# Feed-forward token planes at one residue modulo 512 bytes, with a copied high part for the narrow products

## The reference

```python
def swiglu_ffn(h, w_gate, w_up, w_down):
    return (jax.nn.silu(h @ w_gate) * (h @ w_up)) @ w_down

for l in range(DEPTH):                     # DEPTH = 2, x is 256 tokens by 1024
    h = rms_norm_2(x, ffn1_norm[l])
    x = x + 0.5 * swiglu_ffn(h, ffn1_w_gate[l], ffn1_w_up[l], ffn1_w_down[l])
    ...                                    # mixer
    h = rms_norm_2(x, ffn2_norm[l])
    x = x + 0.5 * swiglu_ffn(h, ffn2_w_gate[l], ffn2_w_up[l], ffn2_w_down[l])
```

## Time and profile before

| | before |
|---|---|
| median of 3 runs | 2394.99 us (2394.8 to 2395.54) |
| the profiled execution | 2395.84 us |
| its span, first to last instruction | 2393.7 us |
| mean granted TensorE clock in the span | 0.999 |

### The profile page before, as it was taken

How to read it: one execution, slowest core, us unless ns; L and a number is a source line. 1 busy time by engine, 2 the same in 40 slices (tenths; PEclk the granted TensorE clock), 3 DMA queues, 4 the chain that set the end, 5 groups by cost and what they waited for, 6 DMA issues and landing times.

```text
span 2393.7 us, 34175 instructions
## 1 busy us (share of the span) xinstructions
PE 2371.1 (99%) x12542; PEld 2012.4 (84%) x12542; DVE 1877.3 (78%) x1961; ACT 1439.7 (60%) x1474; POOL 14.3 (1%) x34
## 2 busy tenths in 40 slices
PE   8999999999999999999999999999999999999998
PEld 7788899888888888888888888888888888897887
DVE  7767786678888888888889898677966677788766
ACT  6645455467777777777777776555254454544444
POOL 1000000000000000000000010000000000000000
PEclk9999999999999999999999999999999999999999
DMA  8375233459999999999999996853455666533663
GB/s 302 111 258 177 70 131 141 152 202 376 382 379 348 381 379 378 348 381 377 380 348 378 381 395 249 281 180 124 132 188 181 194 229 230 177 128 123 199 192 126
DMA packets 315953, 603.73 MB, mean 252 GB/s; under 512 B 9121, under 2 KB 135201, under 8 KB 315553
## 3 DMA queue, kind: packets, MB, share of 16 engines
q1 hardware_dynamic: 314160, 592.70, 69.9%
q10 hardware_dynamic: 1136, 7.87, 0.8%
q0 software_dynamic: 576, 2.10, 0.2%
HBM read 597.91 MB, written 8.91 MB: 254 GB/s over the span
## 4 chain that ended last, share of the span: by engine, by line
PE 94%; DVE 3%; ACT 1%; DMA 1%; DVEq 1%; issue 0%; SPq 0%; ACTq 0%
PE bank L217 20%; PE bank L219 19%; PE bank L218 19%; PE bank L1229 17%; PE bank L1234 8%; PE bank L3526 1%; PE bank L2968 1%; PE bank L3453 1%; PE bank L2243 1%; PE bank L2253 1%; DMA mslot<-in_e_w_in 1%; PE bank L2943 1%; PE bank L1727 1%; PE bank L1070 0%; PE bank L2162 0%
## 5 line engine op out<-in xcount | busy, mean ns | idle before, releaser
L3218 DVE TENSOR_TENSOR weights_lo<-mslot,weights_hi 128x2048 fp32r<-128x2048 f32 x336 | 767.5, 2291 | 112.8 <-ACT weights_hi L3111 112.1
L3111 ACT ACTIVATE weights_hi<-mslot 128x2048 fp32r<-128x2048 f32 x336 | 644.1, 1920 | 212.9 <-PE bank L219 212.8
L1229 PE MATMUL bank<-x_parts,weights_hi 128*128 128x512 f32 x1760 | 510.3, 393 | 1.9 <-DVE x_parts L933 1.9
L1383 DVE TENSOR_TENSOR weights_lo<-scratch,weights_hi 128x2048 fp32r<-128x2048 f32 x165 | 377.2, 2289 | 164.4 <-ACT weights_hi L1376 164.4
L1229 PEld LDWEIGHTS bank<-x_parts,weights_hi 128*128 128x128 f32 x1760 | 325.2, 188 | 71.3 <-DVE x_parts L933 2.4
L217 PE MATMUL bank<-weights_hi,x_parts 128*128 128x512 f32 x920 | 359.7, 391 | 1.0 <-DVE weights_lo L3218 0.7
L217 PE MATMUL bank<-weights_hi,x_pair 128*128 128x512 f32 x896 | 354.8, 396 | 0.2 <-issue 0.2
L219 PE MATMUL bank<-weights_hi,x_pair 128*128 128x512 f32 x896 | 349.8, 390 | 0.0
L218 PE MATMUL bank<-weights_lo,x_pair 128*128 128x512 f32 x896 | 349.3, 390 | 0.0
L218 PE MATMUL bank<-weights_lo,x_parts 128*128 128x512 f32 x888 | 346.1, 390 | 0.0
L1234 PE MATMUL bank<-x_parts,weights_lo 128*128 128x256 f32 x1760 | 343.3, 280 | 0.0
(11 more groups left out here) (551 smaller groups left out, 2625.2 us busy)
## 6 DMA issues: line engine op xcount, KB each, us to landing
mslot<-in_o_moe_w_gate SPq DMA_DIRECT2D x112, 1024.0 KB, 6.4
mslot<-in_o_moe_w_up SPq DMA_DIRECT2D x112, 1024.0 KB, 6.3
mslot<-in_o_moe_w_down SPq DMA_DIRECT2D x112, 1024.0 KB, 6.6
scratch<-in_ffn_w_gate SPq DMA_DIRECT2D x44, 1024.0 KB, 5.4
scratch<-in_ffn_w_up SPq DMA_DIRECT2D x44, 1024.0 KB, 5.4
scratch<-in_ffn_w_down SPq DMA_DIRECT2D x44, 1024.0 KB, 5.2
mslot<-in_o_w_in SPq DMA_DIRECT2D x7, 2048.0 KB, 10.6
scratch<-in_e_ffn_w_gate SPq DMA_DIRECT2D x11, 1024.0 KB, 5.4
```

The costliest lines, as they stand in the source:

```text
L1229: pe.matmul(m.ps[bank + j][:, :].rearrange("p (i t) -> p i t", i=2), hi[:, k, cols(j)], m.x_wide[k], start=(k == 0), stop=False)
L1383: dve.tensor_tensor(m.wlo[to][:, :], m.fslot[i], m.whi[to][:, :], ALU.subtract).then_inc(m.sig["f_lo"], 1)
L3111: act.activation(m.whi[(place + half) % PLACES][:, :], r.slot[slot + half], ACT.Copy).then_inc(s["r_hi"], 1)
L3218: dve.tensor_tensor(m.wlo[i][:, :], r.slot[slot + half], m.whi[i][:, :], ALU.subtract).then_inc(s["r_lo"], 1)
```

## The change

Block 0 stays as it is. For v = 1 to 4 the high plane begins at column `PIECE` = 2048, that is 192 bytes lower, so that both planes have residue 64. In these blocks ScalarE copies the high plane (eight groups of 256 columns) once, after up(0) and ahead of the high part for up(1), to two places at residue 256: three k to a free end of `mix_parts` and five k into `mslot3_parts`. The narrow products of gate(0), up(0) and gate(1) read the high plane (residue 64), those from up(1) on read the copy (residue 256). The stationary operand of the last unit's down product, which lies over the high plane, moves from residue 256 to 64 with it. The order of the products, the counts of products and all semaphores stay.

```diff
+PLANE_AT = [XH_AT] + 4 * [PIECE]
+COPY_SPLIT = 3
+COPY_FRONT, COPY_BACK = 11296, 560
@@ place
+        m.x_copy = [cut(m.mix, COPY_FRONT, COPY_SPLIT, SEQ),
+                    cut(mslot3_parts, KT * HALF + COPY_BACK, KT - COPY_SPLIT, SEQ)]
@@
-    planes = x_all[:, 0:2 * XH_AT].rearrange("p (i t) -> p i t", i=2)
-    m.x_wide = [planes[:, :, k * SEQ:(k + 1) * SEQ] for k in range(KT)]
-    m.f_xl, m.f_xh = cut(x_all, 0, KT, SEQ), cut(x_all, XH_AT, KT, SEQ)
+    planes = [x_all[:, 0:2 * at].rearrange("p (i t) -> p i t", i=2) for at in PLANE_AT]
+    m.x_wide = [[t[:, :, k * SEQ:(k + 1) * SEQ] for k in range(KT)] for t in planes]
+    m.f_xl, m.f_xh = cut(x_all, 0, KT, SEQ), [cut(x_all, at, KT, SEQ) for at in PLANE_AT]
@@ ffn_pe, inner
-            pe.matmul(..., hi[:, k, cols(j)], m.x_wide[k],
+            pe.matmul(..., hi[:, k, cols(j)], m.x_wide[v][k],
+        def narrow_tokens(u, k):
+            if v == 0 or isinstance(u, int) and (u == 0 or u == 1 and kind == "gate"):
+                return m.f_xh[v][:, k, :]
+            return m.x_copy[0][:, k, :] if k < COPY_SPLIT else m.x_copy[1][:, k - COPY_SPLIT, :]
-                last = pe.matmul(m.ps[bank + j][:, 0:SEQ], lo[:, k, cols(j)], m.f_xh[:, k, :],
+                last = pe.matmul(m.ps[bank + j][:, 0:SEQ], lo[:, k, cols(j)], narrow_tokens(u, k),
@@ ffn_hidden
-        pair = [t[:, KT - 2:KT, :].rearrange("p k t -> p (k t)") for t in (m.f_xh, m.f_xl)]
+        pair = [t[:, KT - 2:KT, :].rearrange("p k t -> p (k t)") for t in (m.f_xh[v], m.f_xl)]
@@ ffn_act
     up(0)
+    if v > 0:
+        act.activation(m.x_copy[0], m.f_xh[v][:, 0:COPY_SPLIT, :], ACT.Copy)
+        act.activation(m.x_copy[1], m.f_xh[v][:, COPY_SPLIT:KT, :], ACT.Copy)
+        act.drain()
     ffn_hi(act, m, v, "up", 1)
```

More of the change, by code:

```diff
@@ L933, in ffn_entry_low @@
         dve.scalar_tensor_tensor(m.f_xl[:, k, :], turned(m, u, k),
-                                 gain[:, k:k + 1], m.f_xh[:, k, :], ALU.mult, ALU.subtract).then_inc(s["n_xl"], 1)
+                                 gain[:, k:k + 1], m.f_xh[m.splits[u]][:, k, :], ALU.mult, ALU.subtract).then_inc(s["n_xl"], 1)
 def ffn_entry_dve(dve, m, u, gain, v, scale):
@@ L1027, in tokens @@
             act.wait_ge(s["n_tr"], rows_turned(m, u) + k // 2 + 1)
-            last = act.activation(m.f_xh[:, k, :], turned(m, u, k), ACT.Copy, scale=gain[:, k:k + 1])
+            last = act.activation(m.f_xh[m.splits[u]][:, k, :], turned(m, u, k), ACT.Copy, scale=gain[:, k:k + 1])
             if k % 2 == 1:
@@ L1228, in wide @@
         def wide(j, k):
-            pe.matmul(m.ps[bank + j][:, :].rearrange("p (i t) -> p i t", i=2), hi[:, k, cols(j)], m.x_wide[k],
+            pe.matmul(m.ps[bank + j][:, :].rearrange("p (i t) -> p i t", i=2), hi[:, k, cols(j)], m.x_wide[v][k],
                       start=(k == 0), stop=False)
+        def narrow_tokens(u, k):
+            if v == 0 or isinstance(u, int) and (u == 0 or u == 1 and kind == "gate"):
+                return m.f_xh[v][:, k, :]
+            return m.x_copy[0][:, k, :] if k < COPY_SPLIT else m.x_copy[1][:, k - COPY_SPLIT, :]
         def narrow(j, ks):
             for k in ks:
-                last = pe.matmul(m.ps[bank + j][:, 0:SEQ], lo[:, k, cols(j)], m.f_xh[:, k, :],
+                last = pe.matmul(m.ps[bank + j][:, 0:SEQ], lo[:, k, cols(j)], narrow_tokens(u, k),
                                  start=False, stop=(k == KT - 1))
@@ L1285, in down_part @@
         hi, lo = parts(ffn_place(v, "down", NU - 1 if final else None), D)
-        hh, hl = ffn_hidden(m, last=final)
+        hh, hl = ffn_hidden(m, v, last=final)
         cols, tok = slice(half * HALF, (half + 1) * HALF), slice(t * P, (t + 1) * P)
@@ L1335, in ffn_pe, with ffn_hidden @@
         norm_pe(pe, m, u_out, 0)
-def ffn_hidden(m, last):
+def ffn_hidden(m, v, last):
     if last:
-        pair = [t[:, KT - 2:KT, :].rearrange("p k t -> p (k t)") for t in (m.f_xh, m.f_xl)]
+        pair = [t[:, KT - 2:KT, :].rearrange("p k t -> p (k t)") for t in (m.f_xh[v], m.f_xl)]
     else:
@@ L1468, in hidden @@
     def hidden(u, last=False):
-        hh, hl = (flat(t) for t in ffn_hidden(m, last))
+        hh, hl = (flat(t) for t in ffn_hidden(m, v, last))
         for j, cols in enumerate(halves):
```

## The result

| | before | after |
|---|---|---|
| median (8 runs each, alternating) | 2395.38 us (2394.61 to 2396.08) | 2401.98 us (2401.00 to 2403.86) |
| ratio, 95% interval | | 1.0028 [1.0019, 1.0037] |
| span of the profiled execution | 2393.7 us | 2398.9 us |

The account below looks back on a forecast made before the run. TensorE fills the feed-forward blocks, so time is the sum of product pitches. Terms -4.1 (wide), -0.4 (last down), +0.6 (early narrow), others zero, sum to -3.9 us: 2394.99 to 2391.1, range 2387.6 to 2396.6.

Parts of the forecast that it names:

- Step (1): Wide products of gate and up, both planes at residue 64, take 0.2267 us each: 0.097 us saved per pair, 4.1 us.
- The second route: Check on the wide products' gain: mean durations 393 against down's 390 ns, 3 ns x 352 x 4 = 4.2 us.
- Step (2): Narrow products from up(1) on keep residue 256 and pitch 0.1156: zero, bounds 3.1 us saved or 2.9 us lost.
- C: Rival: the phase persists, pairs gain nothing, only the gate's opening run gains slightly: -0.2 us, 2394.8; chance 0.20.
- E: Rival: each wide-to-narrow meeting of residues 64 and 256 costs 0.0066 us: +4.6 us, 2399.6; chance 0.13.
- Step (3): Narrow products of gate(0), up(0), gate(1) go to residue 64: 192 products by 3 ns, 0.6 us lost.
- Step (4): Last down's stationary operand goes to residue 64: 24 products a block from 0.2310 to 0.2267, 0.4 us gained in four blocks.
- Step (5): ScalarE's copy ahead of up(1), about 2.1 us, is covered by idle time: cost nothing; other bound 8.8 us in all.
- Step (6): The entry's ScalarE writes of the high plane only change address: zero; a tenth on each would be 0.3 us a block.
- B: Rival: wide and narrow products all at their lowest pitch, 0.2267 and 0.1133: -7.0 us, 2388.0; chance 0.20.
- D: Rival: residue affects no pitch, as TensorE's two SBUF ports are independent: 0.0 us, 2395.0; chance 0.07.

Follow-up runs that it names:

- the run with the planes back: Changed kernel with the high plane of blocks 1 to 4 back at residue 256, copies kept: 2395.5 us beside 2395.68 for the kernel before, ratio 0.9999.
- The copy-less kernel: Changed kernel without the copy, both planes at residue 64, all narrow products reading the high plane: 2402.32 us, ratio 1.0028 to the kernel before.
- The residue scan: Six single runs with high plane, copies or low plane at other residues by block: 2400.93 to 2403.73 us, beside 2395.4 to 2395.6 for the kernel before.

## Why the prediction was wrong

**What bounds the kernel** was right: in these blocks the time is the sum of the pitches. So was the remark that something is carried from one product to the next; its reading as a phase between the reads of the moving operand and of the next weights is not shown by any run.

The group of wide products over the whole span hides what happened, as the earlier trace rows do for before:

```profile
L1234 PE MATMUL bank<-x_parts,weights_hi 128*128 128x512 f32 x1760 | 513.1, 394 | 1.9 <-DVE x_parts L938 1.9
```

394 ns where it was 393: a duration ends at a modelled end, and only the starts show the pitch.

**Step (1), wide products at 0.2267 everywhere, -4.1 us: the step that failed.** It took "the nearest row for that is down's 0.2267" as a property of the residue. Up's opening has 0.2267 before and after, with the high plane at 256 and at 64, so it told nothing of the pairs. The gate's opening went to 0.2322, not to 0.2267, and the pairs to 0.350 in place of 0.342. Where the step forecast 97 ns less for a gate and up, they take 108 ns more (11047 to 11155). In each term what was read off was one place of a cycle. The second route, 393 less 390 ns, compared durations, which don't show the pitch.

**Step (2), narrow products unchanged, 0 within 3 us either way.** The residue of their operand is unchanged and their pitch isn't: up's run went from 0.1133 to 0.1178, the upper of the two bounds, 9 x 4.4 = 40 ns of up's 63. (The two bounds, 3.1 and 2.9 us, are one term rounded in two ways: 32 products by 2.25 ns, 42 times, is 3.0.) The mistake was to price wide and narrow products apart, when the run freezes at the place where the pairs leave the cycle.

**Down behind a gate, which no step priced**, lost 45 ns in each of eight units a block and 19 ns in one, 1.5 us in four blocks. The prediction looked at the entry to down only in the rivals C and E, as a measure for something else. The question to ask was what follows each changed product.

**Step (3)**: the narrow products of the first three groups have a mean duration of 283 ns, as said, but a duration isn't a price. By the starts, a block comes 0.13 us later to its first down in blocks 1 and 2 and 0.16 in block 4, where 0.14 was forecast for narrow products alone; the wide ones have changed in it too, so the agreement is partly luck. (In block 3 a wait at the entry hides it.) **Step (4)**: the 20 down products at the end of block 2 take 1929.99 - 1925.46 = 4.53 us, as forecast, against 4.62 in the earlier trace rows. These are the row of the narrow products on `x_parts` in block 2 of the changed kernel, and the end of that block in order of time:

```profile
L1244 PE MATMUL bank<-x_parts,weights_lo 128*128 128x256 f32 x48 | 8.7, 283 | 0.0
```
```profile
1925.46 0.39 PE L222 MATMUL bank<-weights_hi,x_parts 128*128 128x512 f32 x1
...
1929.99 0.39 PE L224 MATMUL bank<-weights_hi,small_parts 128*128 128x512 f32 x1
```

**Step (5), the copy at nothing**, was right, and the run with the planes back shows it by itself. ScalarE, VectorE and TensorE in block 1:

```profile
1487.39 0.85 ACT L1429 ACTIVATE mix_parts<-x_parts 128x768 fp32r<-128x768 f32 x1
1488.13 1.27 ACT L1430 ACTIVATE mslot_parts<-x_parts 128x1280 fp32r<-128x1280 f32 x1
1489.52 1.92 ACT L1386 ACTIVATE weights_hi<-scratch 128x2048 fp32r<-128x2048 f32 x1
1491.95 2.28 DVE L1393 TENSOR_TENSOR weights_lo<-scratch,weights_hi 128x2048 fp32r<-128x2048 f32 x1
1497.88 2.20 PE L1234 MATMUL bank<-x_parts,weights_hi 128*128 128x512 f32 x9
```

The copy takes 2.1 us, the high part behind it ends at 1491.44 (1491.9 was said), VectorE takes it up at 1491.95, and up(1) begins with no idle time before it. **Step (6)** has nothing in the traces against it.

**The rivals.** E had the sign and nearly the price: 16 x 0.0066 = 0.106 us per gate and up, measured 63 + 45 = 108 ns. It fell short of the 6.6 us mainly by down. But its mechanism, a price for each meeting of 64 and 256, is not what happens. The copy-less kernel has no such meeting and costs 148 ns. And the cost doesn't follow their number: with 8, 7, 6, 5 and 4 pairs the changed layout has 18, 16, 14, 12 and 10 meetings of a wide product and the narrow one behind it per gate and up, and costs 95, 108, 64, 64 and 20 ns over before's 11047. The number was a coincidence, and at 0.13 the chance was too low for a change of phase, which can go either way. C was right that a phase persists, and wrong that it would leave things as they are. B's state, all at the lowest, occurs in no run.

D, that residues have no effect, is refuted: one high plane at 64, 128, 192 or 256 gives 11195, 11171, 11227 or 11047 ns for the same 32 wide and 32 narrow products, each narrow one reading that plane. The Trainium skill, SBUF — State Buffer, section "Who interferes with whom", has TensorE's port for the moving operand and its port for weight loads as independent. The prediction took from that that no residue changes a pitch. The residue scan doesn't agree with this reading: the sums differ by up to 3% (11047 to 11379). Whether the two ports disturb each other or one of them is slower at some residues by itself, no run here shows.

**What stays open.** The pitches are described here, not derived. What makes the cycle of 234, 231, 228 isn't shown, nor why the changed layout never has the run at 113.3. That the interplay is one between reads of the moving operand and of the weights is only argued: the weights' own residue was 64 in every gate and up of every run. Moving the weights is the run that is missing.

## What to carry to other kernels

On a stretch that TensorE fills, compare start-to-start distances at single positions of the stream, not means per kind of instruction: 393 against 394 ns in the view of groups hid 12 ns in every second wide product. A change of address and a change of order can't be priced apart; try the few orders that the dependencies allow again after each change of layout, and look at what the next group pays. And a low pitch seen in one place is a property of its neighbours too, so it doesn't forecast a gain in another place.

## What the runs showed of the hardware

- The pitch of float32r products depends on where the planes that they read as moving operand lie: in one order, seven pairs, the same 16 wide and 16 narrow products of a gate take 5523 (low/high 88/256) to 5760 ns (256/320) at a clock of 1.00. For the high plane only the residue modulo 256 bytes counts.
- With wide and narrow ones in turn, the pitches form a cycle (234, 231, 228 with 113, 116, 117 on before's layout; 239, 227 with 117 on the changed one). On before's layout the run of narrow ones behind it stays at 113.3 or at 117.7 to its end, by where the cycle was left; on the changed one it is at 117.7 in all orders tried.
- A place in the cycle is handed on. On these two layouts the next product's first wide or down products run at 227; or at 231 and 229 in turn for the whole opening; or at 232, 232, 231 or 239, 232, 231 and then 227; or at 233, 233, 236, 224, 231, 236, 228. Which of them goes by how many pairs the one ahead had. The eight to fifteen narrow products between don't wipe it out.
- The move of 8 bytes, low plane from 64 to 72, costs 193 ns per gate and up (11240 against 11047, in block 0 of one run).
